# Projections and attention of a second block interleaved, four heads at a time

## What is computed

```python
for l in range(DEPTH_2):                      # l = 0: layer a, l = 1: layer b
    if l < N_A:                               # a: 16 heads of q, k and v, causal attention
        h = rmsnorm_2(x, attn_norm[l])
        q, k, v = jnp.split(h @ w_qkv_a[l], 3, axis=-1)
        q = partial_rope(heads(q, N_HEADS), cos, sin)
        k = partial_rope(heads(k, N_HEADS), cos, sin)
        o = moba_attention(to_bhsd(q), to_bhsd(k), to_bhsd(heads(v, N_HEADS)))
    else:                                     # b: 4 heads of k and v, shared by 16 of q; window 128, sinks
        ...
        o = swa_sink_attention(q, shared_k, shared_v, sinks_b[i])
    x = x + o.transpose(0, 2, 1, 3).reshape(B_, S_, N_HEADS * HEAD_DIM) @ w_o
    x = x + conv_ffn(rmsnorm_2(x, ffn_norm[l]), w_up[l], conv_w[l], conv_b[l], w_down[l])
return rmsnorm_2(x, final_norm)
```

## Time and profile before

| | us |
|---|---|
| median of 3 runs | 1722.07 |
| lowest, highest | 1720.96, 1734.61 |
| the profiled execution | 1734.19 |
| its span, first to last instruction | 1732.4 |
| PE, VectorE, ScalarE busy in it | 1535.8, 1038.3, 769.7 |
| layer a: projections, then attention to the last addition to x | 1023.7 to 1108.7, to 1185.5 |
| layer b: the same | 1393.2 to 1437.3, to 1513.3 |

### The profile page before, as it was taken

The page is one execution under the profiler, slowest core; times in us unless marked ns, Lnnn a source line. Parts: engine busy times, 40 slices in busy tenths (PEclk is TensorE's granted clock), DMA queues, the critical chain, the costliest instruction groups (busy, mean ns, idle before and its releaser), DMA issues.

```text
span 1732.4 us, 22946 instructions
## 1 busy us (share of the span) xinstructions
PE 1535.8 (89%) x8428; PEld 1125.5 (65%) x8428; DVE 1038.3 (60%) x2079; ACT 769.7 (44%) x1648; POOL 272.4 (16%) x260
## 2 busy tenths in 40 slices
PE   7899998969988898887878879898999987899997
PEld 3799657845444333332323249788999986899997
DVE  1345326376666666776666447535777766467774
ACT  2444334224444444444444353545555545455553
POOL 0000000044433444444444300000000000000000
PEclk9699999989999999999999999879999998899997
DMA  7154444399999999999999934304555431244551
GB/s 289 68 195 171 170 146 146 122 377 423 427 427 427 426 427 427 426 428 426 427 427 427 428 147 146 122 1 160 181 173 190 169 122 49 73 163 178 187 176 73
DMA packets 59986, 431.76 MB, mean 249 GB/s; under 512 B 6784, under 2 KB 7296, under 8 KB 7552
## 3 DMA queue, kind: packets, MB, share of 16 engines
q0 software_dynamic: 36864, 268.45, 36.8%
q1 hardware_dynamic: 22176, 160.44, 25.7%
q10 hardware_dynamic: 864, 1.80, 0.3%
HBM read 429.62 MB, written 1.05 MB: 249 GB/s over the span
## 4 chain that ended last, share of the span: by engine, by line
PE 44%; DMA 20%; ACT 7%; DVE 6%; issue 2%; POOL 1%; ACTq 0%; POOLq 0%; DVEq 0%; SPq 0%
PE banks L594 18%; DMA arena<-in_peer_uv,experts 17%; PE banks L922 11%; PE banks L1028 7%; DMA tok_b<-in_peer_uv,experts 2%; DVE wlow L1480 2%; PE banks L809 2%; ACT diag L1300 2%; PE banks L626 1%; PE banks L783 1%; ACT scores L1208 1%; PE banks L648 1%; DVE arena L1836 1%; ACT L1292 1%; ACT L1285 1%
## 5 line engine op out<-in xcount | busy, mean ns | idle before, releaser
L922 PE MATMUL banks<-arena,diag 128*128 128x512 f32 x824 | 403.6, 626 | 95.2 <-ACT diag L1300 95.0
L922 PEld LDWEIGHTS banks<-arena,diag 128*128 128x128 f32 x824 | 150.4, 195 | 336.6 <-ACT diag L1300 200.3
L1836 DVE CUSTOM_DVE_ANT_0 arena<-arena,scores 128x1024 f32<-128x1024 f32 x206 | 252.6, 1226 | 183.8 <-DMA arena<-in_peer_uv,experts 182.8
L1480 DVE TENSOR_TENSOR wlow<-wring,whigh 128x1024 fp32r<-128x1024 f32 x234 | 275.4, 1220 | 128.9 <-ACT whigh L1071 128.8
L1442 POOL DMA_INDIRECT arena<-in_peer_uv,experts x206 | 217.4, 1055 | 650.0 <-DVE experts L1800 349.6
L1071 ACT ACTIVATE whigh<-wring 128x1024 fp32r<-128x1024 f32 x234 | 233.8, 1048 | 140.9 <-DMA wring<-in_w_qkv_a 33.4
L594 PE MATMUL banks<-f_high,whigh 128*128 128x256 f32 x720 | 205.8, 286 | 16.1 <-DVE f_low L1516 10.7
L594 PE MATMUL banks<-f_low,whigh 128*128 128x256 f32 x720 | 204.5, 284 | 0.0
L594 PE MATMUL banks<-f_high,wlow 128*128 128x256 f32 x720 | 204.4, 284 | 0.0
L1292 ACT ACTIVATE dots<-dots 128x1 f32<-128x1 f32 x256 | 51.4, 201 | 287.2 <-DVE dots L1836 286.9
L594 PE MATMUL banks<-a_high,whigh 128*128 128x256 f32 x552 | 166.1, 301 | 13.8 <-DVE a_low L1488 8.1
(11 more groups left out here) (233 smaller groups left out, 2525.1 us busy)
## 6 DMA issues: line engine op xcount, KB each, us to landing
wring<-in_w_up SPq DMA_DIRECT2D x44, 1024.0 KB, 4.8
wring<-in_w_mod SPq DMA_DIRECT2D x24, 1024.0 KB, 4.8
wring<-in_w_down SPq DMA_DIRECT2D x22, 1024.0 KB, 4.8
wring<-in_w_in SPq DMA_DIRECT2D x17, 1024.0 KB, 4.8
wring<-in_w_qkv_a SPq DMA_DIRECT2D x12, 1024.0 KB, 4.9
wring<-in_peer_w_q SPq DMA_DIRECT2D x8, 1024.0 KB, 4.9
wring<-in_w_mix_out SPq DMA_DIRECT2D x4, 1024.0 KB, 4.8
wring<-in_w_o_a SPq DMA_DIRECT2D x4, 1024.0 KB, 4.8
```

What stands on the lines that cost most here:

```text
L922: mm = nc.tensor.matmul(banks[:, 2 + 2 * b + half, :], diag[:, n % DIAGS, :], ring[n % RING][:, D + half * 512:D + (half + 1) * 512], star ...
L1480: V.tensor_tensor(low, w, high.bitcast(F32), ALU.subtract).then_inc(w_split, 1)
L1836: V.tensor_tensor_reduce(out=ring[n % RING][:, 0:D], in0=ring[n % RING][:, 0:D], in1=h2tok[:, b, :], scale=1.0, scalar=0.0, op0=ALU.mult, ...
```

## The change

- The groups of attention in layers a and b are numbered four heads at a time, both query blocks of four heads in turn, and each group ends by itself: division, turning back and the high and low part are done for four heads of a query block, eight times a layer instead of four.
- Time is cut into slots, in each of which PE makes half a chunk of projections (24 matmuls). `starts` says in which slot a group's scores are made: 6, 7, 12, 13, 18, 19, 24, 25 in layer a, 7 to 14 in layer b. Two slots later its probabilities are turned, three later v is weighed, four later it is turned back, five later VectorE makes the low part.
- The order of the chunks becomes q, k, v of the same four heads, four times, in layer a; k, v, then four of q in layer b.
- The last slots have no projections left; parts of the output projection (`wo_early`) stand in their place, the rest behind all slots.
- ScalarE rounds, and VectorE lowers, a chunk at the end of each odd slot from the fourth on: chunk n + 2 in the slot in which chunk n is read. The scaling of x comes at the end of slot 5.
- Banks: two for projections instead of three, one for rotations, two for scores instead of four, two for turning, one for the weighed sums. The heads' high and low parts get places of their own (`o_high`, `o_low`), and the divided heads a buffer `otok`.
- The first block's attention keeps its order; its functions are only shared.

The functions `turn_probs`, `weigh`, `turn_heads`, `maxima`, `normalise`, `exps`, `probs_out`, `heads_out` and `low_out` do what their namesakes did, for the heads of one group. The core of the diff (PE, then ScalarE, then VectorE):

```diff
+        def starts(which, n):
+            return 6 * (n // 2) + 6 + n % 2 if which == 1 else 7 + n
+        TURN, WEIGH, BACK = 2, 3, 4
...
-        proj2 = [[("q", n) for n in range(4)] + [("k", n) for n in range(4)] + [("v", n) for n in range(4)],
-                 [("k", 0)] + [("q", n) for n in range(4)] + [("v", 0)]]
+        proj2 = [[(kind, n) for n in range(4) for kind in "qkv"],
+                 [("k", 0), ("v", 0)] + [("q", n) for n in range(4)]]
...
-                srcs = [chunk_of(a["w_qkv_a_2"], i) for i in range(12)]
+                srcs = [chunk_of(a["w_qkv_a_2"], 4 * part + n) for n in range(4) for part in range(3)]
             else:
-                srcs = ([chunk_of(a["w_kv_b_2"], 0)] + [chunk_of(a["w_q_b_2"], i) for i in range(4)] +
-                        [chunk_of(a["w_kv_b_2"], 1)])
+                srcs = [chunk_of(a["w_kv_b_2"], i) for i in range(2)] + [chunk_of(a["w_q_b_2"], i) for i in range(4)]
...
+            def score(plan, g):
+                if plan["which"] == 0:
                     if g["n"] >= 2:
                         pe.wait_ge(score_read, g["n"] - 1)
-                    width = g["blocks"] * P
-                    each = len(g["heads"]) // 2
-                    for j, h in enumerate(g["heads"]):
...
+            def attention_slot(plan, slot):
+                at = plan["at"]
+                if slot - BACK in at:
+                    turn_heads(plan, at[slot - BACK])
+                if slot - WEIGH in at:
+                    weigh(plan, at[slot - WEIGH])
+                if slot - TURN in at:
+                    turn_probs(plan, at[slot - TURN])
+                if slot in at:
+                    score(plan, at[slot])
...
+            def wo_part(l, g, j, pieces):
+                c = wo_chunks[l][g]
+                pe.wait_ge(w_split, 2 * c["split"] + j + 1)
+                for k in range(2 * pieces[0], 2 * pieces[-1] + 2):
+                    if k % 2 == 0:
+                        pe.wait_ge(o_ready, 2 + 8 * l + k + 2)
+                    for n, (w, x) in enumerate(((whigh, o_high), (whigh, o_low), (wlow, o_high))):
+                        mm = nc.tensor.matmul(
+                            banks[:, g, j * T:(j + 1) * T],
+                            w[:, c["slot"], :].rearrange("p (k n) -> p k n", k=KT)[:, k, j * P:(j + 1) * P],
+                            x[:, k, :], start=(j == 0 and k == 0 and n == 0), stop=(k == KT - 1 and n == 2),
+                            skip_group_check=True)
+                return mm
+            def wo_early(l, slot):
+                if l == 0:
+                    if slot < 6:
+                        wo_part(0, slot // 2, slot % 2, (0, 1, 2))
+                elif 0 < slot < 7:
+                    for g in ((2,), (0, 1))[slot % 2]:
+                        for j in range(2):
+                            wo_part(1, g, j, ((slot - 1) // 2,))
             pe.wait_ge(proj_read, 16)
...
-                    if r >= 2:
-                        pe.wait_ge(roped2, r - 1)
-                    nc.tensor.matmul(banks[:, 3 + r % 2, :], const[:, C_ROT2:C_ROT2 + P], raw[:, r % 2, :],
+                    if r >= 1:
+                        pe.wait_ge(roped2, r)
+                    nc.tensor.matmul(banks[:, 2, :], const[:, C_ROT2:C_ROT2 + P], raw[:, r % 2, :],
...
+                plan = plans[1 + l]
+                for slot in range(plan["slots"]):
+                    n, j = divmod(slot, 2)
+                    if n < len(proj2[l]):
+                        project(n, j)
+                    else:
+                        if slot == 2 * len(proj2[l]):
+                            pe.wait_ge(proj2_read, m)
+                            pe.wait_ge(roped2, r)
+                        wo_early(l, slot - 2 * len(proj2[l]))
+                    if j == 0:
+                        rotate()
+                    if l == 1 and slot == 4:
+                        pe.wait_ge(roped2, 9)
+                        for kv in range(KV_HEADS_2):
+                            nc.tensor.matmul(banks[:, 5 + kv // 2, (kv % 2) * T:(kv % 2 + 1) * T],
+                                             const[:, C_DUP + (kv % 2) * P:C_DUP + (kv % 2 + 1) * P], k2[:, kv // 2, :],
+                                             start=True, stop=True).then_inc(dup2_made, 1)
+                    if l == 1 and slot == 7:
+                        pe.wait_ge(dup2_read, 1)
+                    attention_slot(plan, slot)
                 pe.wait_ge(roped2, r)
-                attention(1 + l)
+                for g in range(4):
+                    for j in range(2):
+                        mm = wo_part(l, g, j, (3,) if g < 3 else (0, 1, 2, 3))
+                    mm.then_inc(wo_made, 1)
                 slots, f0 = ffn_plan[l]["slots"], l * FF_STEPS
...
+            def attention_slot(plan, slot):
+                at = plan["at"]
+                if slot - BACK in at:
+                    heads_out(plan, at[slot - BACK])
+                if slot - TURN in at:
+                    probs_out(plan, at[slot - TURN])
+                if slot in at:
+                    exps(plan, at[slot])
...
+                plan = plans[1 + l]
+                for slot in range(plan["slots"]):
+                    n, j = divmod(slot, 2)
+                    if j == 1 and n < len(proj2[l]):
+                        projected(n)
+                    if l == 1 and slot == 4:
+                        act.wait_ge(dup2_made, 4)
+                        copy(flat(kdup2[:, :, :]), banks[:, 5:7, :].rearrange("p b n -> p (b n)")).then_inc(dup2_read, 1)
+                    attention_slot(plan, slot)
+                    if j == 1 and 1 <= n <= len(proj2[l]):
                         round_next()
-                if l == 1:
-                    act.wait_ge(dup2_made, 4)
...
+            def attention_slot(plan, slot):
+                at = plan["at"]
+                if slot - BACK - 1 in at:
+                    low_out(plan, at[slot - BACK - 1])
+                if slot - WEIGH in at:
+                    normalise(plan, at[slot - WEIGH])
+                if slot in at:
+                    maxima(plan, at[slot])
...
+                plan = plans[1 + l]
+                for slot in range(plan["slots"]):
+                    n, j = divmod(slot, 2)
+                    if j == 0 and 1 <= n <= len(proj2[l]) and proj2[l][n - 1][0] != "v":
+                        rope(n - 1)
+                    attention_slot(plan, slot)
+                    if j == 1 and 1 <= n <= len(proj2[l]):
                         low_next()
-                    if l == 0 and n == 2:
+                    if l == 0 and slot == 5:
                         x_out()
-                attention(1 + l)
+                m += len(proj2[l])
```

More of the change, by code:

```diff
@@ new lines, in weigh @@
+            def weigh(plan, g):
+                blocks = g["blocks"]
+                if g["begins"] and g["finish_before"] is not None:
+                    pe.wait_ge(o_scaled, g["finish_before"] + 1)
+                if plan["which"] > 0:
+                    pe.wait_ge(proj2_read, (None, 3 * (g["first"] // 4) + 3, 14)[plan["which"]])
+                for n, (quad, e) in enumerate(g["quads"]):
+                    pe.wait_ge(quad_copied, quad + 1)
+                    for b in range(4):
+                        at = 4 * n + b
+                        h = g["heads"][at // blocks]
+                        kb = at % blocks
+                        col = (h - g["first"] if plan["which"] > 0 else h) * HD
+                        mm = nc.tensor.matmul(banks[:, g["bank"], col:col + HD], probsT[:, e % 4, b * P:(b + 1) * P],
+                                              plan["v"][:, kb, plan["vcol"](h):plan["vcol"](h) + HD],
+                                              start=(kb == 0), stop=(kb == blocks - 1))
+                    mm.then_inc(pv_made, 1)
@@ new lines, in turn_heads, with attention_first @@
+            def turn_heads(plan, g):
+                pe.wait_ge(o_scaled, g["finish"] + 1)
+                bank = bank_of(plan, g["finish_quad"])
+                heads = tmp[:, g["qb"], :] if plan["which"] == 0 else otok[:, g["n"] % 2, :]
+                for t in range(g["finish_heads"] // 2):
+                    mm = nc.tensor.transpose(banks[:, bank, t * P:(t + 1) * P], heads[:, t * P:(t + 1) * P], ident)
+                mm.then_inc(quad_turned, 1)
+            def attention_first():
+                plan = plans[0]
+                groups = plan["groups"]
@@ L841, in _ @@
             pe.wait_ge(roped, 3)
-            attention(0)
+            attention_first()
             g = 0
@@ L963, in _ @@
                     operand = high_low[2 if l == 1 and kind != "q" else 0]
[L964 to L965 removed]
+                    if j == 0 and m >= 2:
+                        pe.wait_ge(proj2_read, m - 1)
                     if kind == "v":
[L967 to L973 removed]
```

447 lines of the change are left out of this document (207 added, 240 removed).

## The result

| | us |
|---|---|
| before, median of 10 runs (lowest, highest) | 1723.72 (1720.96, 1734.61) |
| after, median of 10 runs (lowest, highest) | 1739.18 (1734.80, 1753.90) |
| ratio, 95% interval | 1.0081 (1.0055 to 1.0106) |
| the profiled execution of after, its span | 1737.76, 1735.9 |

The change makes the kernel 15.5 us slower; 10 were forecast.

A forecast was written before the change was run, and what follows sets the result against it. Projections bound by TensorE, attention by a chain over PE, ScalarE and VectorE; layer a -9.5, layer b +19.7, net +10 us: 1744 against the profiled execution, put at 1732 for the median; own range 1719 to 1741.

The forecast's parts named there:

- The wait for the reciprocal: Layer b's start: v0's scale columns wait for VectorE's low half and reciprocal; PE idles 1404.35 to 1409.9, 5.55 us lost.
- The ends of the scores: Layer b's slots: when each head group's scores end on PE, from queues walked step by step, first score at time 0.
- The gaps of slots 13, 14 and 15: Layer b: early output projection waits for low halves behind maxima on VectorE; PE idles 5.85, 5.35 and 3.1 us.
- first matmul to second score: Layer a's start: second score waits 1.6 us for the scores to be read and ends at 1061.05.
- two periods: Layer a: two periods of six half chunks, rotations and attention, bound by PE, 25.3 us each.
- last period: Layer a: output projection replaces projections; PE waits 0.8 and idles 3.0 us; last score ends at 27.5.
- tail to last low half: Layer a after the last score: maxima, exponentials, weighing, turning and 36 matmuls to the last low half, 16.6 us.
- to the last addition: Layer a's end: 12 matmuls (1.45 us) free the fourth chunk's slot, then 14.8 us kept from the trace of before.
- clock, in the last three: Layer a: gaps of 3.0, 2.4 and 4.3 us slow PE's clock behind them, 4 us in all.
- Rival 1: Both layers: the gaps cost no clock, -13.5 + 11.4, so 1720 us; chance 0.17.
- Rival 2: Layer b: queues don't meet as placed and PE bounds it, 9 us won; 1700 us; chance 0.12.
- Rival 3: Layer b: PE stays at half clock from slot 12 to the last turn, b +34; 1746 us; chance 0.17.

The follow-up runs named there:

- v_late: Changed kernel with layer b's v0 projected third instead of second; layer b 141.0 us against 147.8, kernel 1737.88 us (1 run).
- warm: Changed kernel with 44 additional unused matmuls on PE in layer b's wait for the reciprocal; layer b 144.3 us, kernel 1736.95 us (1 run).
- best_b: Changed kernel with layer b's v0 third and early output projection behind attention, and a third of two chunks' early projection left to the end in both layers; 1713.52 us.
- a_only: Kernel before with the change in layer a alone, layer b ordered as before; 1718.33 us, ratio to before 0.9963.
- less_early: Changed kernel with a third of the second and third chunks' early output projection (24 matmuls) left to the end in both layers; 1734.70 us (1 run).

## Why the prediction was right in kind, and where it was off

**Layer b: right, step by step.** From the layer's first projection matmul the working gave 131.4 us at full clock and 8.3 of clock, 139.7; the trace has 142.1 (1375.7 to 1517.8).
- The wait for the reciprocal: 5.55 us predicted, 5.7 measured; the slow half chunk behind it 1.84, and v_late shows the wait as a cause, and warm the gap as what slowed the half chunk.
- To the end of the first score: 38.7 + 1.9 predicted, 41.5 measured. The layer's first chunk took 8.15 us, not the 7.66 of the earlier trace rows.
- The ends of the scores, predicted at 0, 4.8, 10.6, 17.8, 25.4, 34.6, came at 0, 5.0, 10.8, 18.1, 25.6, 34.4. The seventh and eighth, predicted at 46.35 and 56.9 plus 1.9 and 3.8 of clock, came at 48.6 and 61.2. Going through three in-order queues from single durations held within 0.5 us.
- The gaps of slots 13, 14 and 15: 5.85, 5.35 and 3.1 predicted; waits of 5.7 and 5.8 measured, and a third of 3.4 (1478.4 to 1481.9 in the chain).
- From the eighth score to the last low half 19.6 + 1.7 predicted, 22.0 measured; from there to the last addition 17.15 predicted, 17.4 measured.

The sum is not right by cancellation: its four stretches (to the first score, to the eighth, to the last low half, to the last addition) are all short, by 0.9, 0.5, 0.7 and 0.2 us.

**Layer a: the mechanism right, its gain mis-sized.** The working gave 148.3 us at full clock and 4 of clock, 152.3; the trace has 156.2. The gaps came as predicted: PE waited 2.7, 2.5 and 4.3 us for the heads, the probabilities and the fourth weight chunk, where 3.0, 2.4 and 4.3 were in the working. These terms of the sum were too small:

| term | predicted | measured |
|---|---|---|
| first matmul to second score | 37.3 | 38.4 |
| two periods | 50.6 | 51.8 |
| last period | 27.5 | 29.85 |
| tail to last low half | 16.6 | 18.8 |
| to the last addition | 16.25 | 17.4 |
| clock, in the last three | 4 | |
| sum | 152.3 | 156.2 |

The first chunk took 8.21 us; it took 7.49 in the trace of before and 7.48 in best_b's, whose code is the same up to there, and 8.3 to 8.5 in the other seven. So 0.7 of the first line belongs to the execution: in its first 4 us the granted clock was 0.50 in after and 0.66 in before and best_b. The period is PE's own sum and not a wait: PE waited 0.4 us in two periods. The half chunks behind another kind of matmul took 2.93 and 3.07 us, not 2.88, and block 0's weighing 1.08, not 0.87; such changes of kind come many times in a period now, and I had priced each piece by a row without them. The last line is two things. The 12 matmuls to the first free slot took 1.83 us with their start (1149.24 to 1151.07), not 1.45. And from there to the last addition it took 15.56, not 14.8: three weight loads are asked for within 2.9 us and the second takes 7.19 us, where it took 4.96 before, with 2.9 us between them. I had kept the stretch of before whole, although my own step let the slots come free closer together. That the spacing matters is borne out over all traces, though not to the tenth. Counted from the first request to the last addition, the eleven layer ends with 1.4 us between the requests took 15.5 to 16.1 us; of the nine with 2.9 us between them five took 14.65 to 14.8, three 15.35 to 15.45, and layer b of a_only 16.2.

**The feed-forward: not zero.** It took 1.4 us more, which was put at nothing. The granted clock differs. The windows of 8 us behind layer a's last addition, in before and in after:

```profile
1185.55:1193.55 8.00, 7.07 (x54) 6.92 (x55) 3.16 (x8) 4.31 (x8) 0.00 (x0) 1.00 0.00 0
1166.63:1174.63 8.00, 7.06 (x46) 7.07 (x47) 3.17 (x9) 4.27 (x7) 0.00 (x0) 0.79 0.00 0
```

The 100th matmul of the stretch comes 1.4 us later in after than in before, and from there on they keep step. v_late and warm, with the same layer a, have 1.00 there and 200.6 and 200.7 us, so the loss comes and goes between executions of the same code, and it is not shown to come from the change.

**The conversion to the median.** The working gave +10 and took 12 off the profiled execution for what lies outside the terms. The first block explains that: layer a begins 13.3 us later in the profiled execution of before than in that of after. Measured +15.5 in the medians and +16.9 in the stretches. Of the 6.7 us between the working's 10.2 and those 16.9, 3.9 are layer a's shortfall, 2.4 layer b's excess and 0.4 the feed-forward parts and the rest. The 1739.18 lie near the upper end of the forecast's own range, 1719 to 1741. Put at the layers' beginnings in the trace of before, the last additions came at 1179.9 and 1535.3, behind the 1172 to 1177 and the 1525 to 1533 that were named as signs.

**The rivals.** Rival 1 (gaps cost no clock) falls by warm. Rival 2 (layer b bound by PE) falls by the three gaps; of the 9 us that it would have won in layer b, best_b reached 5.6 with another order. Rival 3 (half clock from slot 12 to the end) falls too: behind 24 matmuls at 4.48 us the next 12 took 1.43 us (1488.89) and the next 24 took 3.10 (1492.37), full clock, both in the chain of waits of after. The rule of the Trainium skill ("TensorE: Matmul & The Clock Gate", part 4, PE-mode transpose) that stood beside it would have kept the clock low there; the trace does not show that, with transposes thin among other matmuls, and no run here has them alone.

## What to carry to other kernels

When work of two kinds is interleaved on one in-order engine, put what is ready first: the filler that waits for a late producer must stand behind the critical chain's next step, not ahead of it. Moving it within the slot was worth 16.8 us here, with not one instruction more or less. Count a gap on PE like those here, of 3 to 6 us, twice, once as idle and once as the slow matmuls behind it, and judge each layer of a change by itself: the same change won in the layer with 12 chunks to interleave and lost in the one with 6. And measure a saving at the end of one part together with what follows it: 2.6 of the 3.1 us that less_early won in layer b came back behind it.

## What the runs showed of the hardware that I had not expected

- Three loads of 1024 KB asked for within 2.9 us: the second took 7.2 us from issue to landing. With 2.9 us between them it took 4.96 in before, and 5.5 in less_early.
- 44 matmuls of no use in a gap of 5.7 us kept the granted clock at 1.00, and the half chunk behind them took 3.07 us instead of 4.72.
- Behind the gaps of layer b the first matmuls lost 1.84, 2.6, 1.5 and 1.6 us against 0.12 us a matmul. Behind the 1.5 only 12 of them follow, and the turning back and weighing after them lost 0.9 more (0.43 and 1.54 us, where 0.22 and 0.84 were taken at 1490.31). So a gap of 3.4 us cost 1.6 and gaps of 5.7 and 5.8 cost 1.8 to 2.6.
- The same code ran its first 8 us behind layer a at a granted clock of 0.79 in some executions and of 1.00 in others, worth 1.4 us.
